# The first transfer of a decoder block, cut into two halves of 64 rows on two queues

## What is computed

```python
u = rmsnorm(h, ln_mix[i])
proj = u @ w_in[i]
x_lru, g_lru, q, k, v = jnp.split(proj, split_at, axis=-1)
y_lru = rglru(causal_dwconv(x_lru, conv_w[i], conv_b[i]), ...) * jax.nn.gelu(g_lru)
y_att = moba_attention(rmsnorm(q, q_gain[i]), rmsnorm(k, k_gain[i]), v, slopes)
h = h + jnp.concatenate([y_lru, y_att], axis=-1) @ w_out[i]
u = rmsnorm(h, ln_ffn[i])
g_up, v_up = jnp.split(u @ w_up[i], 2, axis=-1)
h = h + (jax.nn.gelu(causal_dwconv(g_up, ffn_conv_w[i], ffn_conv_b[i])) * v_up) @ w_down[i]
h = h + jax.nn.sigmoid(rmsnorm(h, ln_ple[i]) @ w_ple_gate[i]) * (p[i] @ w_ple_proj[i])
```

## Time and profile before

| | us |
|---|---|
| median of 3 runs | 634.01 (633.53 to 634.43) |
| the profiled execution | 634.09 |
| its span in the trace | 632.3 |
| TensorE busy | 627.9 |
| DVE, ScalarE, GpSimd busy | 438.4, 337.3, 362.1 |

### The profile page before, as it was taken

How to read it: one execution, slowest core, us unless ns; L and a number is a source line. 1 busy time by engine, 2 the same in 40 slices (tenths; PEclk the granted TensorE clock), 3 DMA queues, 4 the chain that set the end, 5 groups by cost and what they waited for, 6 DMA issues and landing times.

```text
span 632.3 us, 7947 instructions
## 1 busy us (share of the span) xinstructions
PE 627.9 (99%) x2885; PEld 521.5 (82%) x2885; DVE 438.4 (69%) x650; ACT 337.3 (53%) x492; POOL 362.1 (57%) x267
## 2 busy tenths in 40 slices
PE   9999999999999999999999999999999999999997
PEld 7887788888888888888888888888888888888886
DVE  3692499978748797769734477697354677989574
ACT  5779953878836455546333345453343364457341
POOL 6684433743307537499664454996644559963370
PEclk9999999999999999999999999999999999999999
DMA  8742335471103644303546223045462222652022
GB/s 297 289 136 98 101 100 133 123 203 61 41 1 121 242 171 167 100 1 102 132 137 233 97 100 101 1 119 128 154 230 76 99 95 93 170 172 100 34 84 83
DMA packets 22934, 77.80 MB, mean 123 GB/s; under 512 B 2672, under 2 KB 3184, under 8 KB 22640
## 3 DMA queue, kind: packets, MB, share of 16 engines
q1 hardware_dynamic: 21456, 72.45, 34.3%
q0 software_dynamic: 1296, 4.72, 4.0%
q10 hardware_dynamic: 144, 0.13, 0.1%
HBM read 64.83 MB, written 4.19 MB: 109 GB/s over the span
## 4 chain that ended last, share of the span: by engine, by line
PE 99%; DVE 0%; issue 0%; POOL 0%; POOLq 0%
PE psum L1519 30%; PE psum L1521 30%; PE psum L1520 30%; PE psum L1715 2%; PE psum L1701 1%; PE psum L1661 1%; PE psum L1565 1%; PE psum L1568 1%; PE psum L1573 1%; PE psum L1598 1%; PE psum L1848 1%; PE psum L1631 1%; PE psum L1616 1%; PE psum L1682 0%; PE psum L1558 0%; PE psum L1658 0%
## 5 line engine op out<-in xcount | busy, mean ns | idle before, releaser
L505 POOL TENSOR_TENSOR wlo<-raw,whi 128x512 fp32r<-128x512 f32 x82 | 112.9, 1377 | 192.3 <-ACT whi L591 191.9
L1521 PE MATMUL psum<-uhi,wlo 128*128 128x512 f32 x488 | 189.8, 389 | 0.0
L1520 PE MATMUL psum<-ulo,whi 128*128 128x512 f32 x488 | 189.8, 389 | 0.0
L1519 PE MATMUL psum<-uhi,whi 128*128 128x512 f32 x488 | 189.8, 389 | 0.0
L506 POOL TENSOR_TENSOR wlo<-raw,whi 128x512 fp32r<-128x512 f32 x82 | 117.6, 1434 | 0.0
L591 ACT ACTIVATE whi<-raw 128x1024 fp32r<-128x1024 f32 x78 | 81.9, 1054 | 58.0 <-PE psum L1521 57.3
L1520 PEld LDWEIGHTS psum<-ulo,whi 128*128 128x128 f32 x488 | 91.6, 188 | 19.1
L1519 PEld LDWEIGHTS psum<-uhi,whi 128*128 128x128 f32 x488 | 91.6, 188 | 19.1
L1521 PEld LDWEIGHTS psum<-uhi,wlo 128*128 128x128 f32 x488 | 91.6, 188 | 18.9
L837 ACT ACTIVATE tmp<-psum,vec 128x512 f32<-128x512 f32 x24 | 16.6, 690 | 84.3 <-DVE psum L1293 84.3
L1364 DVE TENSOR_TENSOR ws<-raw,held 128x1024 f32<-128x1024 f32 x24 | 47.1, 1987 | 9.3 <-POOL elo L557 9.1
(11 more groups left out here) (253 smaller groups left out, 1183.9 us busy)
## 6 DMA issues: line engine op xcount, KB each, us to landing
raw<-in_weights SPq DMA_DIRECT2D x94, 512.0 KB, 3.3
held<-in_weights SPq DMA_DIRECT2D x12, 512.0 KB, 5.7
wlo<-ws POOLq DMA_DIRECT2D x6, 512.0 KB, 5.9
xtok<-in_x SPq DMA_DIRECT2D x4, 512.0 KB, 8.8
out<-first SPq DMA_DIRECT2D x1, 2048.0 KB, 8.7
back<-out SPq DMA_DIRECT2D x1, 2048.0 KB, 7.7
first<-in_x_t SPq DMA_DIRECT2D x7, 256.0 KB, 7.1
raw<-in_weights SPq DMA_DIRECT2D x7, 256.0 KB, 7.1
```

The costliest lines, as they stand in the source:

```text
L505: nc.gpsimd.tensor_tensor(wlo[s][:, 0:CW // 2], raw[s][:, 0:CW // 2], whi[s][:, 0:CW // 2].bitcast(F32), ALU.subtract)
L1519: mm(o, ahi, bhi, start=start, stop=False, skip_group_check=shared)
L1520: mm(o, ahi, blo, start=False, stop=False, skip_group_check=shared)
L1521: return mm(o, alo, bhi, start=False, stop=stop, skip_group_check=shared)
```

## The change

The lead transfer is issued as two transfers of 64 rows: rows 0 to 63 from SyncE's queue, still on `block_in[0]`, and rows 64 to 127 from ScalarE's queue, as ScalarE's first instruction, on a new semaphore `lead_half`. DVE, ScalarE and TensorE wait for both.

```diff
-            sp.dma_start(first[:, 0:LEAD + T], lead_in[:, :]).then_inc(block_in[0], 16)
+            sp.dma_start(first[0:DH, 0:LEAD + T], lead_in[0:DH, :]).then_inc(block_in[0], 16)
...
+            act.dma_start(first[DH:P, 0:LEAD + T], lead_in[DH:P, :]).then_inc(lead_half, 16)
             act.wait_ge(ident_ok, 1)
             nc.scalar.activation(ones_r[:, :], ones[:, :], ACT.Copy).then_inc(ones_ok, 1)
+            act.wait_ge(lead_half, 16)
             norm_x(0)
...
             dve.wait_ge(block_in[0], 16)
+            dve.wait_ge(lead_half, 16)
             V.tensor_scalar(wg[:, :], lead[:, KD:KD + P], lead[:, 0:1], None, ALU.mult).then_inc(wg_ok, 1)
...
                     pe.wait_ge(block_in[0], 16)
+                    pe.wait_ge(lead_half, 16)
                     mm(bank[0][:, :], wg[:, :], res[:, 0, :], start=True, stop=False)
```

More of the change, by code:

```diff
@@ L311, in build @@
         half_hi, half_lo, xl_done = sem("half_hi"), sem("half_lo"), sem("xl_done")
-        wg_ok = sem("wg_ok")
+        wg_ok, lead_half = sem("wg_ok"), sem("lead_half")
         ident_ok, dist_ok, pool_step = sem("ident_ok"), sem("dist_ok"), sem("pool_step")
```

## The result

| | before | after |
|---|---|---|
| median of 18 runs, us | 633.96 (633.53 to 634.43) | 634.57 (634.22 to 636.75) |
| ratio, 95% interval | | 1.0019 (1.0012 to 1.0025) |
| span of the profiled execution | 632.3 | 632.6 |

The changed kernel is slower, by 0.19% in the ratio, 1.2 us. The median, 0.6 us higher, tells only half of it: the 18 times fall into two groups, 11 from 634.22 to 634.61 and 7 from 636.12 to 636.75, with nothing between. The kernel before has one group. I had forecast no change, a range of 633.5 to 635.0, and 0.90 for "within 0.2%": the median lies in the range and the mean, 635.22, above it; the ratio is just inside 0.2%, but its interval is clear of 1, so the change is real.

The account below looks back on a forecast made before the run. TensorE's row of matmuls was taken as the bound, fillers and lead transfer ending together. Issue 0, SyncE 0, waits 0.05 and landing 0 gave +0.05 us on 634.09, about 634.1 us; range 633.5 to 635.0.

Parts of the forecast that it names:

- What bounds the kernel: Whole kernel: TensorE busy 627.9 of 632.3 us; at the start fillers and lead transfer end together, near zero slack.
- Part 1: ScalarE's queue at the start: the added issue, about 0.37 us, delays the table load but stays covered; cost 0.
- Part 2: SyncE's queue at the start: first transfer half as large, issue pitch expected unchanged (0.46 us each); cost 0.
- Part 3: DVE, TensorE and ScalarE at the start: waiting for one more semaphore costs 0 to 0.1 us, taken as 0.05.
- Part 4: Lead transfer: both halves landed at 4.17 us as before, give or take 0.1; cost 0.
- my own sign of being wrong: Start of the changed profile: DVE starting after 4.6 us and L1558 following it would show the forecast wrong.
- Rival B: Lead transfer: the halves serialize and land at 5.4 us, 1.25 late; 634.7 to 635.3 us, 8%.
- The clock: TensorE's start: lower level, 1.2 GHz against 2.4, until near 6.1 us; time gained or lost before that worth half.
- rival C: TensorE's start: 1.25 us of idleness keeps the lower clock level to about 10.8 us; +3.0, 637.1 us, 5%.
- rival A': Lead transfer: issues follow each other or ScalarE's queue starts slowly, lower rows up to 0.4 us late; 634.3 us, 5%.
- The sum on record: Whole kernel: issue 0, SyncE 0, waits 0.05, landing 0 (-0.1 to +0.1), together +0.05 us.
- A: Lead transfer, the forecast itself: both halves land near 4.2 us, 633.6 to 634.6 us, 80%.

## Why the prediction was wrong

- **What bounds the kernel**: right. TensorE's row is all, and the fillers and the lead end together; with the lead late TensorE idled.
- **Part 1, ScalarE's issue hidden**: right in its effect (the cast of `ones` ends near 3, and ScalarE then idles for 2.09 us until the lead lands), wrong in its size, 0.58 for 0.37.
- **Part 2, SyncE's pitch unchanged**: wrong. 0.58 and 0.56 for the first two, so the rest is 0.33 later. It cost little, as argued: half 1 was not late.
- **Part 3, the extra waits**: DVE starts 0.08 after ScalarE, where both had started at 4.17; that is within the 0 to 0.1 given.
- **Part 4, the landing, is the step that failed.** The sum has it at 0 (-0.1 to +0.1) for a landing at 4.17, by the 128 KB stores at the kernel's end. Over the five traces with this cut on two queues it measured 4.86 to 5.20, and my own sign of being wrong, DVE after 4.6 with L1558 behind it, came true. Those stores have 128 rows. The trace before has 64-row transfers too, copies within the on-chip memory (`q_spare[p][upper, :]` from `qT[0][lower, p, :]` and the like); I wrote only that no row shows a 64-row load from HBM, and priced nothing by them. They show the cost in SyncE's queue near 99 to 107 us, full-row issues beside 64-row ones, and a full-row one right behind them:

```profile
98.53 0.33 SPq L367 DMA_DIRECT2D raw<-in_weights  x1
98.90 1.82 SPq L413 DMA_DIRECT2D k_more<-qThi  x3
104.53 1.75 SPq L416 DMA_DIRECT2D qThi<-qTlo  x3
106.32 0.58 SPq L367 DMA_DIRECT2D raw<-in_weights  x1
```

  A full-row issue takes 0.33, three of 64 rows take 1.82 and 1.75, about 0.6 each, and the next full-row one 0.58. This is the very pattern of the changed kernel's start. Their 128 KB took 4.0 us (L413) and 2.3 us (L416) to land, against 1.9 for the stores of the same size on 128 rows. These were the nearest rows for a 64-row transfer. A long issue alone is no sign of 64 rows, though; the same trace has full-row ones of 0.64 to 0.78 us between 5 and 8 us, with no 64-row transfer ahead of them:

```profile
4.98 0.65 SPq L373 DMA_DIRECT2D xtok<-in_x  x1
...
6.36 0.78 SPq L377 DMA_DIRECT2D raw<-in_weights  x1
```

- **Rival B** had the landing at 5.4, by half the rate: the size was near and the mechanism another. The fourth us moved 322 KB against 317 before, so the rate was not halved there; the start was late, and half 1 was not pushed back. Its price through the lead alone was +0.6; the lower group lies at 634.40 in its median, +0.4.
- **The clock** had no term in the sum, only rival C, and here the second step failed. **Rival C** is what happened in 13 of 40 executions. I gave it 5% and 637.1 us; it measured 636.1 to 637.0. The over-price is in the idle time, 0.90 to 1.04 us by the starts and not 1.25, and in the length for which the level stayed low, to 9.1 and not 10.8. Nor does a gap always start the stretch at the lower level over: the level rose near 5.6 in the first trace, with a gap of 0.90. The error was to tie it wholly to B, and to treat its threshold as unknown and far while the sum left no slack at all: with a gate at zero slack, a delay of 0.4 us (rival A') would already have opened a gap.
- The sum on record, +0.05, stands against +0.4 in the lower group (634.40 against 633.96) and +1.2 over the first 18 runs by the ratio. The upper group lies 2.1 above the lower one (636.5 against 634.4), and 0.4 + 13/40 x 2.1 = 1.1 us. The stated 0.90 for "within 0.2%" leaned on A above all. That the ratio, 1.0019, still falls inside 0.2% is luck: A's landing didn't happen, and with somewhat more executions in the upper group it would lie outside.

## What to carry to other kernels

Price a transfer by a row with its own partition count: the trace had the issue of 64 rows at nearly twice the time of 128 (0.6 us against 0.33), far from the place of the edit. Where filler matmuls are cut to end just as the first data lands, lateness costs twice, its own time and, in some executions, a late rise of the clock. With a fifth filler none of 11 runs was in the upper group, and the median stayed as it was; whether it would cost or gain in the kernel before was not measured. When a transfer is added to a queue, follow what stands behind it: slab 1 lost more than the lead had won. And read the single runs where a median and a mean part: here the one moved by 0.6 us and the other by 1.3.

## What was not expected of the hardware

- Issue of a DMA of 64 rows: 0.58 us at the start, on either queue, alone or beside another, and 0.56 to 0.58 for the next issue on SyncE's queue; of 32, 48, 80, 96 and 128 rows: 0.39 to 0.42.
- Landing after the issue: 3.4 us for 388 KB on 128 rows, 3.6 and 4.3 for its halves of 64 rows on two queues, 3.3 and 3.4 for halves of 128 rows on two queues (one trace each).
- The moment at which TensorE's clock level rose differs between executions of one kernel (near 5.6 and near 9.1 us in the changed one), and the granted-clock column of the windows read 1.00 at either level; only the cadence, 0.427 or 0.23 us for a matmul of L1569, shows it.
